# Expert stage with its choices in one piece: GpSimd asks for a row gather only when the third last one it asked for has landed

## The reference

```python
s_top, i_top = lax.top_k(scores, PEER_TOPK)
cand = (s_top[:, :, 0, :, None] + s_top[:, :, 1, None, :]).reshape(tb, PEER_HEADS, PEER_TOPK * PEER_TOPK)
...
best, pos = lax.top_k(cand, PEER_TOPK)
idx = jnp.take_along_axis(cand_idx, pos, axis=-1).reshape(tb, PEER_HEADS * PEER_TOPK)
gate = jax.nn.softmax(best, axis=-1).reshape(tb, PEER_HEADS * PEER_TOPK)
u = jnp.take(expert_u, idx, axis=0)
act = jax.nn.gelu(jnp.einsum("tkd,td->tk", u, hb).astype(jnp.float32), approximate=False)
vv = jnp.take(expert_v, idx, axis=0)
return jnp.einsum("tk,tkd->td", (gate * act).astype(hb.dtype), vv)
```

## Time and profile before

| | |
|---|---|
| median of 3 runs | 2874.39 us (2873.33 to 2880.9) |
| profiled execution | 2878.42 us, its span 2876.8 us |
| PE busy | 2565.4 us (89%) |
| DVE busy | 1576.0 us (55%) |
| ACT busy | 956.6 us (33%) |
| POOL busy | 812.3 us (28%) |
| mean granted TensorE clock | 0.942 |
| gathers | 512, queue q0, 268.47 MB |

### The profile page before, as it was taken

The page is one execution under the profiler, slowest core; times in us unless marked ns, Lnnn a source line. Parts: engine busy times, 40 slices in busy tenths (PEclk is TensorE's granted clock), DMA queues, the critical chain, the costliest instruction groups (busy, mean ns, idle before and its releaser), DMA issues.

```text
span 2876.8 us, 37498 instructions
## 1 busy us (share of the span) xinstructions
PE 2565.4 (89%) x15650; PEld 2143.4 (75%) x15650; DVE 1576.0 (55%) x3013; ACT 956.6 (33%) x1526; POOL 812.3 (28%) x668
## 2 busy tenths in 40 slices
PE   7999999998999999999989999998987757567677
PEld 7998998988999989999979978876873323223232
DVE  5447985425445447975345443344146576556754
ACT  4344644414434435554224421622012112112111
POOL 0005770000000017740000000000036666666664
PEclk9999999999999999999999999998988978788898
DMA  6565772034544555751035544431468999999997
GB/s 195 190 173 118 192 177 74 1 121 147 185 152 154 184 146 145 179 147 59 31 104 190 182 127 146 132 117 44 146 248 319 377 354 363 365 367 393 359 367 277
DMA packets 324731, 557.35 MB, mean 194 GB/s; under 512 B 16200, under 2 KB 245586, under 8 KB 324562
## 3 DMA queue, kind: packets, MB, share of 16 engines
q1 hardware_dynamic: 250834, 286.48, 33.7%
q0 software_dynamic: 73728, 268.47, 24.4%
HBM read 553.85 MB, written 1.05 MB: 193 GB/s over the span
## 4 chain that ended last, share of the span: by engine, by line
PE 70%; DVE 18%; issue 5%; another core or an unknown queue 3%; ACT 2%; POOL 1%; DMA 1%; SPq 0%; DVEq 0%; POOLq 0%
PE bank L332 15%; PE bank L392 8%; PE bank L393 8%; PE bank L394 8%; PE bank L2327 7%; DVE proj L2279 3%; PE banks_to L392 3%; PE banks_to L393 3%; PE banks_to L394 3%; DVE banks_to L916 3%; PE banks_to L1095 2%; PE banks_to L332 2%; DVE gdn_conv L1001 2%; PE bank L1095 2%
## 5 line engine op out<-in xcount | busy, mean ns | idle before, releaser
L392 PE MATMUL bank<-operand_hi,weights_high 128*128 128x256 f32 x2432 | 689.7, 284 | 24.0 <-DVE cnv_dw_cols L577 15.7
L393 PE MATMUL bank<-operand_lo,weights_high 128*128 128x256 f32 x2432 | 686.0, 282 | 0.0
L394 PE MATMUL bank<-operand_hi,weights_low 128*128 128x256 f32 x2432 | 684.2, 281 | 0.0
L392 PEld LDWEIGHTS bank<-operand_hi,weights_high 128*128 128x128 f32 x2432 | 461.6, 190 | 27.7 <-DVE cnv_dw_cols L577 16.1
L394 PEld LDWEIGHTS bank<-operand_hi,weights_low 128*128 128x128 f32 x2432 | 463.2, 190 | 0.0
L393 PEld LDWEIGHTS bank<-operand_lo,weights_high 128*128 128x128 f32 x2432 | 462.9, 190 | 0.1
L372 POOL TENSOR_TENSOR weights_low<-weights,weights_high 128x1024 fp32r<-128x1024 f32 x128 | 308.5, 2448 | 489.7 <-ACT weights_high L342 489.4
L2327 PE MATMUL bank<-proj,residual 128*128 128x512 f32 x548 | 274.0, 653 | 143.0 <-issue 94.0
L342 ACT CAST weights_high<-weights 128x1024 fp32r<-128x1024 f32 x392 | 386.1, 1046 | 0.0
L386 DVE TENSOR_TENSOR weights_low<-weights,weights_high 128x1024 fp32r<-128x1024 f32 x264 | 308.0, 1221 | 128.0 <-ACT weights_high L342 128.0
L2327 PEld LDWEIGHTS bank<-proj,residual 128*128 128x128 f32 x548 | 113.7, 210 | 300.5 <-issue 248.2
(11 more groups left out here) (409 smaller groups left out, 3622.2 us busy)
## 6 DMA issues: line engine op xcount, KB each, us to landing
weights<-in_ffn_w_in SPq DMA_DIRECT2D x88, 1024.0 KB, 5.1
weights<-in_mix_w_in SPq DMA_DIRECT2D x64, 1024.0 KB, 11.4
weights<-in_ffn_w_out SPq DMA_DIRECT2D x44, 1024.0 KB, 4.9
weights<-in_w_in SPq DMA_DIRECT2D x24, 1024.0 KB, 5.4
weights<-in_cnv_w_o SPq DMA_DIRECT2D x8, 1024.0 KB, 6.0
weights<-in_gdn_w_o SPq DMA_DIRECT2D x8, 1024.0 KB, 5.4
weights<-in_mix_w_out SPq DMA_DIRECT2D x8, 1024.0 KB, 5.3
weights<-in_peer_w_q SPq DMA_DIRECT2D x8, 1024.0 KB, 5.5
```

The costliest lines, as they stand in the source:

```text
L392: t.matmul(out, w_hi, x_hi, start=start, stop=False, skip_group_check=skip)
L393: t.matmul(out, w_hi, x_lo, start=False, stop=False, skip_group_check=skip)
L394: return t.matmul(out, w_lo, x_hi, start=False, stop=stop, skip_group_check=skip)
```

## The change

GpSimd keeps a list of the landings of all gathers that it has asked for. Before it asks for another, it waits until the third last of them has landed, so that at most three are under way, the new one included. The list runs through u and v gathers alike. The waits for free homes and for the indices stay as they were, and so do all instructions of the other engines and the order of the gathers.

```diff
-GROUP, U_ROWS, V_ROWS = 8, 12, 15
+GROUP, U_ROWS, V_ROWS, IN_FLIGHT = 8, 12, 15, 3
...
-def pool_rows(X, m, S, K, i, homes, landed, freed, table):
+def pool_rows(X, m, S, K, i, homes, landed, freed, table, asked):
...
             X.pool.wait_ge(*freed.at(*row_of(r - len(homes))))
         elif block is not None:
             X.pool.wait_ge(*S.used.at(block))
+        if len(asked) >= IN_FLIGHT:
+            X.pool.wait_ge(*asked[-IN_FLIGHT])
         at = bass.IndirectOffsetOnAxis(ap=K.index[n % 2][:, p * GROUP + s:p * GROUP + s + 1], axis=0)
         landed[r % len(homes)].by(X.gpsimd.indirect_dma_start(out=home, out_offset=None, in_=table, in_offset=at), r)
+        asked.append(landed[r % len(homes)].at(r))
...
 def pool_experts(X, m, S, K, io):
+    asked = []
     for i in range(GROUPS):
-        pool_rows(X, m, S, K, i, K.u, S.u_in, S.dotted, io["peer_u_2"][0])
-        pool_rows(X, m, S, K, i, K.v, S.v_in, S.summed_v, io["peer_v_2"][0])
+        pool_rows(X, m, S, K, i, K.u, S.u_in, S.dotted, io["peer_u_2"][0], asked)
+        pool_rows(X, m, S, K, i, K.v, S.v_in, S.summed_v, io["peer_v_2"][0], asked)
```

## The result

The changed kernel took 3123.5 us (3120.0 to 3126.3, median of 4 runs), the kernel before 2875.5 us beside it: a ratio of 1.0859, 95% interval 1.0839 to 1.0878. The forecast was 3013 us within 2890 to 3110: the right direction, and 110 us too little.

A forecast was written before the change was run, and what follows sets the result against it. Gathers at 1.42 us each, paced by the DMA engines plus stops from DVE's late steps, bound the last stage. The closed loop adds +150, the end -12: net +138 on 2874.4, 3013 us, range 2890 to 3110.

The forecast's parts named there:

- the length of the loop: GpSimd asks, rows land, GpSimd sees it and asks again: 5.2 us for three gathers, 1.73 us each.
- the lone gather: A gather almost alone in the earlier trace: last packets 3.9 us after issue, taken as the loop's lower bound.
- the second gather of a bunch: Gather after a pause, asked at 2261.23 and used by waiting DVE at 2266.41: 5.18 us, source of the 5.2 us.
- the stage: The 480 gathers from 2169 us on: 832 us forecast against 681.6 before, +150 us.
- Five or six are under way: Gathers in flight before the change: 6.80 us to land at 1.24 us between requests, 5.5, so the wait would hold.
- stay in the climbing part: With at most two gathers seen, DMA engines would stay near 300 GB/s, 1.7 us for 524,288 B.
- The heavy rival: Gather stage: third-of-a-bunch landing holds, loop 6.39 us, 2.13 us a gather, 3203 us; loops over 5.8 us, chance 0.11.
- The formula of the page: GpSimd-requested DMA: about 2.0 us plus bytes/436e3, 3.2 us here; loop 4.1 us, 1.38 us a gather, 2843 us.
- The short-loop rival: Gathers three deep don't hinder one another: loop 4.2 us, 1.40 us a gather, 2853 us, faster; chance 0.07.
- DVE's late steps: DVE's expert choices start steps 1.5 to 3 us late ("remote") where gathers are dense; should mostly go, worth nothing net.
- the end: After the last gather's issue: TensorE keeps up, done after 5.2 + 1 us instead of 19.1, so -12 us.
- The start: Before 2169 us: slower first 24 gathers, 12 us, lie mostly in pauses for weight slots; counted as 0.

## Why the prediction was right or wrong

**The step that failed** is the length of the loop: the term for GpSimd's start behind the landing was left out. The prediction said of the lone gather that "its signal and GpSimd's start come on top", and then took 5.2 us from the row of the second gather of a bunch as the whole loop. That row ends where DVE starts, and DVE starts at once; GpSimd starts 0.74 us after DVE on the same landing, and no term of the sum stands for that. The prediction also had put the wait instruction at nothing, since it "lies under the 0.94 us of the gather before". That is so where the wait is satisfied (twenty in flight: 1.0000), not where it stops the engine. Its worth, 0.74/3 x 480 = 118 us, covers the 111.7 us by which the stage was forecast too short (+261.7 against +150).

**The landing** was right: 5.2 us forecast, 5.2 the median. It was read from one row, and landings with three in flight spread from 4.2 to 7.6 us, so that it met the median so closely is in part luck. The reason why three in flight land sooner than the 6.80 us of the earlier trace rows holds: landings grow with the number in flight, 4.3, 5.2, 5.7, 5.9, 6.9 us for two to six. "Five or six are under way" in the kernel before was read from one dense moment; on the faster chip its median landing is 16.8 us, some 16.8/1.286 = 13 gathers. That the engines "stay in the climbing part" near 300 GB/s came out at 268, and again the difference is GpSimd's start. Whether the engines also pause between two gathers that are both asked for, as the prediction has it, no run separates from the time in which too few are asked for.

**The heavy rival** (6.39 us a loop, 3203 us, 0.11) gave its bound in the loop 5.8 us. The measured loop, 3 x 1.964 = 5.89 us, is just past it, but not by its mechanism, since the median landing was 5.2 us. It is the forecast's mechanism with a term left out.

**The formula of the page.** The short-loop rival (2853 us) needed a loop below 4.33 us. The lowest median landing of all runs, with only two in flight, is 4.3 us, and GpSimd's start comes on top. The Trainium skill's "DMA: Bandwidth & Descriptors", section "Anatomy of one DMA — SWDGE (gpsimd) path", gives 3.2 us as an estimate for these bytes. With the 0.94 us of the instruction, as the prediction counted it, that is 4.1 us, and the trace agrees where few are under way: 4.0 us is the shortest landing with two in flight and 4.3 the median. What made the forecast from it fail is the growth to 5.2 us with three, and GpSimd's start.

**DVE's late steps.** The outcome was as forecast: with three in flight every one is gone, and in the long stage it was worth nothing, since the gathers set the pace. The reason given was not: on a faster chip the kernel before has none, at 409 GB/s (one trace; on another chip it takes the same 2801 us). Of the two kinds, the slower shows them with five or more in flight (1.43 us a gather) and not with four (1.56) or three. Whether it is the number in flight or the pace that counts was not separated, since the two changed together, and what differs between the chips stays open. What is late can be read, though. One such step in the kernel before (timeline):

```profile
2288.19 0.18 DVE L2224 CAST gdn_conv<-gdn_conv 128x32 f32<-128x32 uint32 x1 [4.98 <-remote]
```

The step before it ends at 2283.22 us; the update of its semaphore is recorded 4.95 us later, and this one starts 0.02 us after that update. Of 59 waits of over 1 us for DVE's own step before, from 2098 us on, 44 have their update in the trace, and all 44 waits end 0.02 us after it. So DVE isn't slow to start and its steps aren't slow: the signal comes late. In the same traces most updates of the gathers' landings are missing (the kernel before has 1767 of 8192, on the faster chip all 8192), which is also why they give no landing times. Whether the two have one cause is not shown.

**TensorE.** Forecast to wait for v rows, it waits for the diagonals (435.8 us in 30 waits). The forecast counted 8.5 us of matmul for a group, taking the 32 matmul records of the earlier trace rows for two groups. They are one: the 32 groups have 1024 such records, two for each of a group's 16 matmuls, and take 15 to 17 us a group at the clock of this stage (0.76 granted in the mean), and the last group's begin only when its weights are there. The end of the stage after, answering to the earlier trace rows:

```profile
3094.64 14.88 PE L2330 MATMUL bank<-weights,residual 128*128 128x512 f32 x28 [16.68 <-ACT residual L2315]
...
3100.18 0.94 POOL L2270 DMA_INDIRECT proj<-in_peer_v,gdn_conv  x1 [1.63 <-DMA weights<-in_peer_v,gdn_conv]
3109.36 1.88 PE L2330 MATMUL bank<-proj,residual 128*128 128x512 f32 x4
```

TensorE is done 11.1 us after the last issue and not 6.2, so the end gives back 8.0 us where 12 were counted.

**The start** was counted at 0 and gave 12.1 us. The late steps are there too, now on ScalarE. Two of its copies in the kernel before, and TensorE's first product of the experts (timeline; the last row is cut off by its window, at 19 of 32 records):

```profile
2121.11 0.58 ACT L433 COPY ffn_gated<-bank 128x512 f32<-128x512 f32 x1 [15.84 <-remote]
...
2132.32 0.58 ACT L2144 COPY gdn_conv<-bank 128x512 f32<-128x512 f32 x1 [10.62 <-remote]
...
2165.36 10.12 PE L2327 MATMUL bank<-proj,residual 128*128 128x512 f32 x19 [3.19 <-ACT residual L2312]
```

and that product in the kernel after:

```profile
2147.72 15.61 PE L2330 MATMUL bank<-proj,residual 128*128 128x512 f32 x32 [3.20 <-ACT residual L2315]
```

No copy of ScalarE waits on "remote" there, and the product comes 17.6 us sooner. GpSimd's stop of 10.18 us for it is gone as well, but that stop isn't made by late steps: the kernel before on the faster chip, which has none, stops 10.33 us for the same product. There the 32nd gather is asked for at 2157.13 us, against 2156.97 in the kernel after, so the 12.1 us are what the late steps had cost this part of the kernel before. The prediction saw late steps only on DVE and counted nothing for them here. In all: +111.7 for the stage, -12.1 at the start, +4.0 at the end, 103.6 us between +138 and +241.6.

## What to carry to other kernels

When a change closes a loop between the engine that asks for transfers and their landing, the pace is (landing + the asking engine's own start behind the signal) / number in flight, and all three terms must be read for that engine: the start of another engine on the same landing (DVE's 0.02 us here) can't stand for the asking engine's (0.76). Read the landing at the number in flight that the change allows, not from the dense flow. Here every bound up to four left the DMA engines short of requests (203, 268 and 322 GB/s for two, three and four, against 409 without a bound); it took six to cost 0.2% and not more.

If a wait must be put in beside another, let the instruction carry the one whose signal comes later: here the order of two waits was worth 54 us at three in flight and 26 at five, though nothing at five on the chip whose pace the late steps set.

## What the runs showed that I had not expected

- A gather on GpSimd starts 0.74 us after DVE has started on the same landing when the wait stands in an instruction of its own, and 0.24 us after it when the gather carries that wait. Where the wait is satisfied the separate instruction costs nothing.
- The same kernel before takes 2875 to 2878 us on some chips and 2801 us on others. The difference, 75 us, lies in the gather stage: 1.42 us a gather with 50-odd waits on "remote" against 1.286 us with none (64 us over 480 gathers), and 12 us at the stage's start. The changed kernel takes 3120 to 3123 us on both kinds, so the same change measures as 1.086 or as 1.113.
- Without a bound, GpSimd asks faster (1.24 us) than the DMA engines serve (1.28 us): on the faster chip the queue simply grows, to 18 gathers at most, and from issue to landing takes 16.8 us in the median without costing anything.
- Where a step is late, its signal is: the semaphore's update comes up to 5.0 us after the step's end (4.96 in the kernel before), and the waiting DVE step starts 0.02 us after the update.
